# Two-layer decoder trunk: every fourth gate/up weight chunk gets its low part from ScalarE's negated high part and an accumulating transfer

## The chip, the core and the metric

One core of a Trainium2 chip runs the whole program: TensorE (PE in the profile) multiplies, VectorE (DVE), ScalarE (ACT) and GpSimd (POOL) work on tiles in SBUF and PSUM, SyncE (SP) issues most transfers, and 16 DMA engines carry them. The metric is the device time of one execution in microseconds (us); lower is better.

## The reference, cut to what matters

```python
def swiglu(h, w_gate, w_up, w_down):
    return (jax.nn.silu(h @ w_gate) * (h @ w_up)) @ w_down
...
for i in range(DEPTH):                  # DEPTH = 2
    h = rms_norm(x, norm_mix[i])
    x = x + mix                         # gla_mixer in layer 0, fox_mixer in layer 1
    h = rms_norm(x, norm_ffn[i])
    x = x + swiglu(h, ffn_w_gate[i], ffn_w_up[i], ffn_w_down[i])
```

`x` has 256 rows of 2048 float32 values. `w_gate` and `w_up` are 2048 x 5632, `w_down` is 5632 x 2048. All weights are float32 and each is read from HBM once.

## The kernel before

**A chunk.** Weights stream through four slots in SBUF. A chunk is 256 rows by 512 columns of a weight matrix (512 KB), laid out as 128 partitions x 1024 floats. Chunk c lives in slot c mod 4 of three buffers: `raw` (as loaded), `w_hi` (rounded to the reduced format `F32R` that TensorE reads in one pass) and `w_lo` (`raw - w_hi`, the remainder). The activations are split the same way (`xt_hi`, `xt_lo`), and each product is made of three matmuls, hi x hi, hi x lo and lo x hi, so a chunk costs TensorE 2 x 2 x 3 = 12 matmuls of 512 columns.

**The steps of a chunk, and what orders them.** Every engine's list is written out by hand and runs in order; semaphores connect them.

1. SP (`load`, L271) issues the load of a chunk into `raw[slot]` once `lo_done` says that the chunk four before it has had its low part made. That is the moment at which `raw[slot]` is free.
2. ACT (`hi`, L603) waits for the load to land and for `chunk_used` of the chunk four before (its `w_hi` and `w_lo` slot is then free), and writes `w_hi[slot]`.
3. DVE (`lo`, L1003) waits for `hi_done` and writes `w_lo[slot]` by a subtraction; `lo_done` rises by 1.
4. PE (`tile`, L358 to L360) waits for `lo_done`, does its 12 matmuls into `acc`, and raises `chunk_used`.

**The gate/up stage.** For layer 0 and layer 1 a SwiGLU has 11 column blocks (`FT`) of 512. A block is a gate tile of 8 chunks and then an up tile of 8 chunks. Around the chunks, ACT applies Silu to the gate sums (L705, after the third `hi` of the up tile), DVE multiplies by the up sums (L1126) and transposes the result in pieces (L1063), and ACT and DVE split it into `ht_hi` and `ht_lo` (L656, L1072). POOL has nothing to do in these blocks. After block 10 (blocks count from 0) comes the layer's down projection. Over both layers these are 352 gate/up chunks and 176 down chunks, the mixers have the other 288, and the program has 816.

Of the kernel before, what the change touches and what calls it, by code (L numbers as in the profile page):

```python
# [76 lines left out]
def build(nc, x, norm_mix, norm_ffn, gla_w_in, gla_w_g2, gla_b_g2, gla_o_gain, gla_w_o,  # L77
# [39 lines left out]
    with ctx:  # L117
# [137 lines left out]
        neg_made = sem("causal_mask_made")  # L255
        fv_done, og_done, pv_mm, rec_done = sem("fox_v_done"), sem("og_done"), sem("pv_product"), sem("rec_done")

        block = ctx.enter_context(nc.Block())

        GAIN_MIX0, GAIN_MIX1, GAIN_FFN0, GAIN_FFN1, GAIN_O, BIAS_G, GAIN_QK = 0, 16, 32, 48, 64, 68, 76  # L260
# [3 lines left out]
        @block.sync  # L264
        def _(sp):
            def load(src, row, col, c, j):

                slot = j % SLOTS

                wait(sp, lo_done, c + (j - SLOTS + 1))  # L270
                sp.dma_start(  # L271
                    raw[:, slot, :].rearrange("p (k n) -> p k n", n=N),
                    src[row:row + KC_CHUNK * P, bass.ds(col, N) if not isinstance(col, int) else slice(col, col + N)]
                    .rearrange("(k p) n -> p k n", p=P)).then_inc(landed[slot], 16)

            def project(src, col0, tiles, c0):

                with sp.Fori(0, tiles // 2) as i:
                    for j in range(2 * CH):
                        load(src, j % CH * KC_CHUNK * P, i * (2 * N) + (col0 + j // CH * N),  # L280
                             Lin(c0, 2 * CH, i), j)

            def swiglu(layer, c_up, c_down):
                with sp.Fori(0, FT) as i:
                    for j in range(2 * CH):
                        load((w_gate, w_up)[j // CH][layer], j % CH * KC_CHUNK * P, i * N,
                             Lin(c_up, 2 * CH, i), j)
                with sp.Fori(0, DT // 2) as i:
                    for j in range(2 * HCH):
                        load(w_down[layer], j % HCH * KC_CHUNK * P, i * (2 * N) + j // HCH * N,  # L290
                             Lin(c_down, 2 * HCH, i), j)

            def load_x(h):
                s = slice(h * KC_CHUNK * P, (h + 1) * KC_CHUNK * P)
                sp.dma_start(xres[:, :, s], x[0, :, s].rearrange("(b p) n -> p b n", p=P)) \
                    .then_inc(x_landed[h], 16)

            x_before = {0: (0,), 1: (1,), 2: (2,), 3: (3,), 4: (4, 5), 5: (6,), 6: (7,)}
            for j in range(2 * CH):
                for h in x_before.get(j, ()):  # L300
                    load_x(h)
                load(gla_w_in[0], j % CH * KC_CHUNK * P, j // CH * N, Lin(C["gla_in"]), j)
            project(gla_w_in[0], 2 * N, 2 * QT + 2 * DT - 2, C["gla_in"] + 2 * CH)
            project(gla_w_o[0], 0, DT, C["gla_o"])
            swiglu(0, C["ffn0"], C["down0"])
            project(fox_w_in[0], 0, 3 * DT, C["fox_in"])
            project(fox_w_in[0], 3 * D + FH, DT, C["fox_in"] + 3 * DT * CH)
            project(fox_w_o[0], 0, DT, C["fox_o"])
            swiglu(1, C["ffn1"], C["down1"])
            for b in range(TB):  # L310
                sp.wait_ge(staged, G["ffn1"] + FT + DT + b)
                sp.dma_start(out[0, b * P:(b + 1) * P, (DT - 1) * N:DT * N], stage[:, b, :]).then_inc(last_stored, 16)
            sp.wait_ge(last_stored, 16 * TB)
# [3 lines left out]
        def _(pe):  # L317
# [9 lines left out]
                last.then_inc(turned, 1)  # L327

            def tile(pair, c, off, hi, lo, chunks=CH, turn_n=None, mid=None, before=None, ready=None,
                     rows_first=False, second=ident):  # L330


                for j in range(chunks):
                    if before is not None:
                        before(j)
                    if ready is not None and j == chunks - 2:
                        pe.wait_ge(tp_hi, ready)
                        pe.wait_ge(tp_lo, ready)
                    if j == 4:
                        if turn_n is not None:  # L340
                            turn(turn_n, second)
                        if mid is not None:
                            mid()
                    if j == 6 and turn_n is not None:
                        wait(pe, tp_hi, turn_n + 1)
                        wait(pe, tp_lo, turn_n + 1)
                    slot = (c.base + off + j) % SLOTS
                    wait(pe, lo_done, c + (off + j + 1))
                    order = [(r, b) for r in range(KC_CHUNK) for b in range(TB)]
                    if rows_first and j == chunks - 1:  # L350
                        order = [(r, b) for b in range(TB) for r in range(KC_CHUNK)]
                    for r, b in order:
                        k = j * KC_CHUNK + r
                        wh = w_hi[:, slot, r * N:(r + 1) * N]
                        wl = w_lo[:, slot, r * N:(r + 1) * N]
                        o = acc[:, pair, b, :]
                        xh, xl = hi[:, k, b * P:(b + 1) * P], lo[:, k, b * P:(b + 1) * P]
                        pe.matmul(o, xh, wh, start=(k == 0), stop=False)  # L358
                        pe.matmul(o, xh, wl, start=False, stop=False)  # L359
                        last = pe.matmul(o, xl, wh, start=False, stop=(k == chunks * KC_CHUNK - 1))  # L360
                        if rows_first and j == chunks - 1 and (r, b) == (KC_CHUNK - 1, 0):
                            last.then_inc(rows_summed, 1)
                    last.then_inc(chunk_used, 1)
# [20 lines left out]
            def out_and_ffn(c_o, g_o, c_up, g_up, c_down, g_down, second):  # L384
# [6 lines left out]
                tile(1, Lin(c_up), CH, xt_hi, xt_lo)  # L391
                with pe.Fori(1, FT) as i:
                    cc = Lin(c_up, 2 * CH, i)
                    tile(0, cc, 0, xt_hi, xt_lo)
                    tile(1, cc, CH, xt_hi, xt_lo)

                pe.wait_ge(tp_hi, g_up + FT - 1)
                pe.wait_ge(tp_lo, g_up + FT - 1)
# [190 lines left out]
        def _(ac):  # L589
# [12 lines left out]
                wait(ac, chunk_used, cj + (1 - SLOTS))  # L602
                nc.scalar.activation(w_hi[:, slot, :], raw[:, slot, :], ACT.Copy).then_inc(hi_done, 1)  # L603

            def tile(c, off, empty, turned_tile=None, mid=None, chunks=CH, after_8=None, swapped_tile=None):

                for j in range(3):
                    hi(c, off + j)
# [1 line left out]
                    empty()  # L610
                for j in range(3, 7):
                    hi(c, off + j)
                if turned_tile is not None:
                    turned_tile()
                if mid is not None:
                    mid()
                hi(c, off + 7)
                if swapped_tile is not None:
                    swapped_tile()
                if chunks > CH:  # L620
# [68 lines left out]
            def out_and_ffn(c_o, g_o, c_up, g_up, c_down, g_down, norm, first, first_turn, after):  # L689
# [19 lines left out]
                tile(Lin(c_up), CH, lambda: silu(None))  # L709
                with ac.Fori(1, FT) as i:  # L710
                    cc = Lin(c_up, 2 * CH, i)
                    tile(cc, 0, None)
                    tile(cc, CH, lambda: silu(i), lambda: turn_h(Lin(g_up - 1, 1, i), Lin(-1, 1, i)))
                for t in range(DT):
                    if g_down is None and t:
                        tile(Lin(c_down), t * HCH, None, chunks=HCH)
# [274 lines left out]
        def _(ve):  # L991
# [5 lines left out]
                chain[0] += 1  # L997
                ve.wait_ge(dve_chain, chain[0])

            def lo(c, j):  # L1000
                slot = (c.base + j) % SLOTS
                wait(ve, hi_done, c + (j + 1))
                nc.vector.tensor_tensor(w_lo[:, slot, :], raw[:, slot, :], w_hi[:, slot, :].bitcast(F32),  # L1003
                                        ALU.subtract).then_inc(lo_done, 1)

            def tile(c, off, empty=None, turned_tile=None, mid=None, chunks=CH, late=None, swaps=None, after_8=None,
                     swapped_tile=None):
                for j in range(8):
                    lo(c, off + j)
                    if j == 2 and empty is not None:  # L1010
                        empty()
                    if j == 3 and late is not None:
# [89 lines left out]
            def out_and_ffn(c_o, g_o, c_up, g_up, c_down, g_down, m, norm, first, first_turn, saved):  # L1102
# [34 lines left out]
                def up_swaps(n):  # L1137
                    return lambda j: swap_h(n, 10 + 2 * j, 2) if j < 3 else None

                tile(Lin(c_up), 2 * CH, lambda: hidden(Lin(0)), swaps=gate_swaps(Lin(g_up)))  # L1140
                tile(Lin(c_up), 3 * CH, None, lambda: turn_h(Lin(g_up), Lin(0)), swaps=up_swaps(Lin(g_up)))
                with ve.Fori(2, FT) as i:
                    cc = Lin(c_up, 2 * CH, i)
                    n = Lin(g_up - 1, 1, i)
                    tile(cc, 0, lambda: hidden(Lin(-1, 1, i)), swaps=gate_swaps(n))
                    tile(cc, CH, None, lambda: turn_h(n, Lin(-1, 1, i)), swaps=up_swaps(n))
                for t in range(DT):
                    if t == 0:
                        n = Lin(g_up + FT - 1)
# [338 lines left out]
        def _(po):  # L1488
# [28 lines left out]
                nc.gpsimd.tensor_copy(xres[:, :, t * N:(t + 1) * N], stage[:, :, :]).then_inc(x_saved, 1)  # L1517


            link(nc.gpsimd.memset(ident[:, :], 0.0))  # L1520
            nc.gpsimd.affine_select(out=ident[:, :], in_=ident[:, :], compare_op=ALU.not_equal, fill=1.0, base=0,
                                    pattern=[[-1, P]], channel_multiplier=1).then_inc(ident_made, 1)
# [43 lines left out]
            for t in range(DT):  # L1566
                save(G["gla_o"] + t, t)
            x_rstd(1)
            for t in range(DT):
                save(G["down0"] + t, t)  # L1570
            po.wait_ge(chunk_used, C["fox_in"])
# [44 lines left out]
            for t in range(DT):  # L1616
                save(G["fox_o"] + t, t)
            x_rstd(3)
            for t in range(DT - 1):
                po.wait_ge(staged, G["ffn1"] + FT + t + 1)  # L1620
                po.dma_start(out[0, :, t * N:(t + 1) * N].rearrange("(b p) n -> p b n", p=P), stage[:, :, :]) \
# [24 lines left out]
```

## Time and profile before

| | |
|---|---|
| time of three runs | 2316.53, 2316.86, 2317.07 us; median 2316.86 |
| the profiled execution | span 2314.9 us from its first to its last instruction; no separate time is listed for it, so it stands 1.96 us below the median |
| PE busy | 2307.5 us (100%) |
| DVE / ACT / POOL busy | 1505.4 (65%) / 1099.5 (47%) / 167.9 (7%) us |
| transfers | 435.80 MB, mean 188 GB/s |

The profile is of one execution. Busy time counts compute instructions alone. "Idle before" is the time for which an engine stood still just before an instruction, and the name behind the arrow is the instruction whose semaphore ended that. Matmuls overlap in the pipeline, so the duration of one is longer than the distance between two starts.

### The profile page before, as it was taken

What the parts mean: (1) busy time and instruction counts of PE and PEld (TensorE: products, weight loads), DVE (VectorE), ACT (ScalarE), POOL (GpSimd) and SP (SyncE); (2) the same over time, 40 slices, a digit from 0 to 9 for tenths busy, and PEclk for the clock granted to TensorE, in tenths of its full rate; (3) what the DMA queues carried; (4) which work ended last, traced back from release to release, by engine and by line L of the source; (5) the groups of instructions that cost most, each with busy time, mean ns of one, the idle gap of its engine ahead of it and who ended that gap; (6) DMA issues with size and microseconds to landing.
All of it is one profiled execution on the core that took longest, in us unless ns stands there. A gap on an engine that the chain in (4) does not pass through costs nothing.

```text
span 2314.9 us, 29817 instructions
## 1 busy us (share of the span) xinstructions
PE 2307.5 (100%) x10416; PEld 1911.8 (83%) x10416; DVE 1505.4 (65%) x1883; ACT 1099.5 (47%) x1417; POOL 167.9 (7%) x206
## 2 busy tenths in 40 slices
PE   9999999999999999999999999999999999999999
PEld 7888788888888888888888888888888888888887
DVE  6988468566666666666578756577666666675443
ACT  6544554444444444444566656445444444444333
POOL 2036110000000000000223200001000000000000
PEclk9999999999999999999999999999999999999999
DMA  7655545666666665555656655455666666656654
GB/s 216 196 168 165 163 164 185 206 192 195 193 190 192 196 190 192 195 195 191 186 169 219 206 178 164 155 179 196 197 193 189 198 191 190 197 191 203 204 198 142
DMA packets 229932, 435.80 MB, mean 188 GB/s; under 512 B 17604, under 2 KB 19752, under 8 KB 229848
## 3 DMA queue, kind: packets, MB, share of 16 engines
q1 hardware_dynamic: 224416, 430.49, 58.6%
q0 software_dynamic: 1040, 3.69, 0.4%
q10 hardware_dynamic: 4392, 0.50, 0.2%
q8 instruction: 53, 0.87, 0.2%
q14 instruction: 31, 0.25, 0.0%
HBM read 432.52 MB, written 2.11 MB: 188 GB/s over the span
## 4 chain that ended last, share of the span: by engine, by line
PE 98%; DVE 1%; ACT 1%; issue 0%; ACTq 0%; POOL 0%; POOLq 0%; DVEq 0%
PE acc L358 32%; PE acc L360 31%; PE acc L359 31%; PE wk L483 1%; DVE w_lo L1003 0%; PE tp L325 0%; PE wk L540 0%; PE tp L550 0%; DVE fox_qkT L1369 0%; ACT w_hi L603 0%; PE wk L372 0%; PE wk L371 0%; PE wk L567 0%; PE wk L568 0%; PE wk L566 0%
## 5 line engine op out<-in xcount | busy, mean ns | idle before, releaser
L1003 DVE TENSOR_TENSOR w_lo<-raw,w_hi 128x1024 fp32r<-128x1024 f32 x816 | 1010.7, 1248 | 665.9 <-ACT w_hi L603 663.4
L603 ACT ACTIVATE w_hi<-raw 128x1024 fp32r<-128x1024 f32 x816 | 858.8, 1060 | 971.2 <-PE acc L360 935.5
L358 PE MATMUL acc<-w_hi,xt_hi 128*128 128x512 f32 x2304 | 902.8, 392 | 2.3 <-DVE w_lo L1003 2.2
L360 PE MATMUL acc<-w_hi,xt_lo 128*128 128x512 f32 x2304 | 896.8, 389 | 0.0
L359 PE MATMUL acc<-w_lo,xt_hi 128*128 128x512 f32 x2304 | 896.6, 389 | 0.0
L358 PEld LDWEIGHTS acc<-w_hi,xt_hi 128*128 128x128 f32 x2304 | 432.5, 188 | 95.6 <-DVE w_lo L1003 3.1
L360 PEld LDWEIGHTS acc<-w_hi,xt_lo 128*128 128x128 f32 x2304 | 432.4, 188 | 90.4
L359 PEld LDWEIGHTS acc<-w_lo,xt_hi 128*128 128x128 f32 x2304 | 432.6, 188 | 89.5 <-issue 1.0
L358 PE MATMUL acc<-w_hi,ht_hi 128*128 128x512 f32 x704 | 273.9, 389 | 0.0
L359 PE MATMUL acc<-w_lo,ht_hi 128*128 128x512 f32 x704 | 273.9, 389 | 0.0
L360 PE MATMUL acc<-w_hi,ht_lo 128*128 128x512 f32 x704 | 273.9, 389 | 0.0
L1063 DVE STREAM_TRANSPOSE ht_raw<-stage 32x256 f32<-32x256 f32 x496 | 216.2, 436 | 9.4
L360 PEld LDWEIGHTS acc<-w_hi,ht_lo 128*128 128x128 f32 x704 | 132.1, 188 | 27.5
L358 PEld LDWEIGHTS acc<-w_hi,ht_hi 128*128 128x128 f32 x704 | 132.1, 188 | 27.4
L359 PEld LDWEIGHTS acc<-w_lo,ht_hi 128*128 128x128 f32 x704 | 132.1, 188 | 27.4
L358 PE MATMUL acc<-w_hi,yt_hi 128*128 128x512 f32 x256 | 99.9, 390 | 0.0
L360 PE MATMUL acc<-w_hi,yt_lo 128*128 128x512 f32 x256 | 99.6, 389 | 0.0
L359 PE MATMUL acc<-w_lo,yt_hi 128*128 128x512 f32 x256 | 99.6, 389 | 0.0
L1517 POOL COPY xres<-stage 128x1024 f32<-128x1024 f32 x12 | 12.5, 1045 | 1076.1 <-DVE stage L1039 1076.1
L1369 DVE STREAM_TRANSPOSE fox_qkT<-stage 32x256 f32<-32x256 f32 x128 | 55.8, 436 | 8.3 <-ACT stage L908 6.3
L359 PEld LDWEIGHTS acc<-w_lo,yt_hi 128*128 128x128 f32 x256 | 48.1, 188 | 10.0
L360 PEld LDWEIGHTS acc<-w_hi,yt_lo 128*128 128x128 f32 x256 | 48.0, 188 | 10.0
(204 smaller groups left out, 935.6 us busy)
## 6 DMA issues: line engine op xcount, KB each, us to landing
raw<-in_ffn_w_gate_dram SPq DMA_DIRECT2D x176, 512.0 KB, 4.3
raw<-in_ffn_w_up_dram SPq DMA_DIRECT2D x176, 512.0 KB, 3.6
raw<-in_ffn_w_down_dram SPq DMA_DIRECT2D x176, 512.0 KB, 4.6
raw<-in_fox_w_in_dram SPq DMA_DIRECT2D x128, 512.0 KB, 4.9
raw<-in_gla_w_in_dram SPq DMA_DIRECT2D x96, 512.0 KB, 4.5
raw<-in_gla_w_o_dram SPq DMA_DIRECT2D x32, 512.0 KB, 4.2
raw<-in_fox_w_o_dram SPq DMA_DIRECT2D x32, 512.0 KB, 3.6
xres<-in_x_dram SPq DMA_DIRECT2D x8, 256.0 KB, 6.5
```

Of the source, the lines that this page charges most:

```text
L358: pe.matmul(o, xh, wh, start=(k == 0), stop=False)
L359: pe.matmul(o, xh, wl, start=False, stop=False)
L360: last = pe.matmul(o, xl, wh, start=False, stop=(k == chunks * KC_CHUNK - 1))
L483: last = pe.matmul(wk[:, b, h * P:(h + 1) * P], ks, qs, start=(kf == 0), stop=(kf == FPH - 1))
L603: nc.scalar.activation(w_hi[:, slot, :], raw[:, slot, :], ACT.Copy).then_inc(hi_done, 1)
L1003: nc.vector.tensor_tensor(w_lo[:, slot, :], raw[:, slot, :], w_hi[:, slot, :].bitcast(F32), ALU.subtract).then_inc(lo_done, 1)
L1063: last = nc.vector.transpose(dst[32 * j:32 * j + 32, :, :, 32 * i:32 * i + 32], src[32 * i:32 * i + 32, :, :, 32 * j:32 * j + 32])
L1369: last = nc.vector.transpose(dst[32 * j:32 * j + 32, :, :, 32 * i:32 * i + 32], src[32 * i:32 * i + 32, :, :, 32 * j:32 * j + 32])
L1517: nc.gpsimd.tensor_copy(xres[:, :, t * N:(t + 1) * N], stage[:, :, :]).then_inc(x_saved, 1)
```

## The change

In gate/up blocks 1 to 10 of both layers, the chunks in slot 3 (every fourth) get their low part in another way. ACT, right after `w_hi`, writes minus the high part of `raw` into `w_lo` (`minus`, the same Copy with scale -1). POOL waits for it and issues a transfer from `raw[3]` to `w_lo[3]` with accumulation, which adds `raw` to what stands there. DVE leaves these chunks out and raises `lo_done` by 2 at slot 2 to keep the count. PE waits for `lo_added` ahead of such a chunk, and SP waits for it before it loads over `raw[3]`, and once before the down projection. SP's loop over the blocks is written out, since its waits are on constants.

```diff
             def swiglu(layer, c_up, c_down):
-                with sp.Fori(0, FT) as i:
+                for i in range(FT):
                     for j in range(2 * CH):
+                        if j % SLOTS == LAST and (i, j) >= (1, 2 * SLOTS - 1):
+                            sp.wait_ge(lo_added, 16 * ((layer * (FT - 1) + i - 1) * ROUNDS + j // SLOTS))
                         load((w_gate, w_up)[j // CH][layer], j % CH * KC_CHUNK * P, i * N,
-                             Lin(c_up, 2 * CH, i), j)
+                             Lin(c_up + 2 * CH * i), j)
+                sp.wait_ge(lo_added, 16 * (layer + 1) * (FT - 1) * ROUNDS)
...
                 for j in range(chunks):
+                    if by_dma is not None and j % SLOTS == LAST:
+                        wait(pe, lo_added, by_dma(off + j))
...
+            def minus(c, j):
+
+                if j % SLOTS == LAST:
+                    nc.scalar.activation(w_lo[:, LAST, :], raw[:, LAST, :], ACT.Copy, scale=-1.0).then_inc(minus_hi, 1)
...
                 for j in range(3, 7):
                     hi(c, off + j)
+                    if by_dma:
+                        minus(c, j)
...
                 hi(c, off + 7)
+                if by_dma:
+                    minus(c, 7)
...
                 for j in range(8):
-                    lo(c, off + j)
+                    if not by_dma:
+                        lo(c, off + j)
+                    elif j % SLOTS != LAST:
+                        lo(c, off + j, 2 if j % SLOTS == LAST - 1 else 1)
...
+            def add_low(layer):
+
+                for k in range((FT - 1) * ROUNDS):
+                    po.wait_ge(minus_hi, layer * (FT - 1) * ROUNDS + k + 1)
+                    po.dma_start(w_lo[:, LAST, :].bitcast(F32), raw[:, LAST, :], accum_op=ALU.add).then_inc(lo_added, 16)
...
             x_rstd(1)
+            add_low(0)
...
             x_rstd(3)
+            add_low(1)
```

`LAST` is 3 and `ROUNDS` is 4, so each layer has 10 x 4 = 40 such chunks, 80 in all.

On ACT, in the loop over blocks 1 to 10, the rows of the first four chunks of a gate tile were these before; a row that holds `chunk_landed_3` is the wait for slot 3's load.

```order
L74 REGISTER_ALU [waits chunk_landed_2]
L603 ACTIVATE w_hi<-raw 128x1024 [waits chunk_used]
L74 REGISTER_ALU [waits chunk_landed_3]
L603 ACTIVATE w_hi<-raw 128x1024 [waits chunk_used]
L74 REGISTER_ALU
L74 REGISTER_ALU [waits chunk_landed_0]
L603 ACTIVATE w_hi<-raw 128x1024 [waits chunk_used]
```

In the changed kernel the same place reads:

```order
L74 REGISTER_ALU [waits chunk_landed_2]
L616 ACTIVATE w_hi<-raw 128x1024 [waits chunk_used]
L74 REGISTER_ALU [waits chunk_landed_3]
L616 ACTIVATE w_hi<-raw 128x1024 [waits chunk_used]
L621 ACTIVATE w_lo<-raw 128x1024
L74 REGISTER_ALU
L74 REGISTER_ALU [waits chunk_landed_0]
L616 ACTIVATE w_hi<-raw 128x1024 [waits chunk_used]
```

The one added row, L621, stands right behind slot 3's high part and waits for nothing of its own.

On SP, the end of a layer's gate/up loads and the first down load now read as follows; before, each of the slot-3 loads waited for `lo_done` alone, and the branch row waited for nothing.

```order
L278 DMA raw<-in_ffn_w_up_dram 128x2x512 [waits lo_done] x3
L278 DMA raw<-in_ffn_w_up_dram 128x2x512 [waits lo_done,low_added]
L298 UNCONDITIONAL_BRANCH [waits low_added]
L298 ISA
L278 ISA [waits lo_done]
L278 DMA raw<-in_ffn_w_down_dram 128x2x512
```

Every fourth load stands behind `low_added` (the name of `lo_added` in the program), with three more loads queued behind it, and the down loads stand behind the last of a layer.

On POOL, between the last step of the reciprocal root for the FFN's norm and the copies of the down projection, the changed kernel has one new group:

```order
L1529 TENSOR_SCALAR psc<-psc 128x2 [waits pool_chain]
L1530 TENSOR_TENSOR rstd<-psc 128x2 [waits pool_chain]
L1550 DMA w_lo<-raw 128x1024 [waits minus_high_made] x40
L1543 COPY xres<-stage 128x2x512 [waits staged] x4
L1605 MEMSET fox_wn 128x848 [waits chunk_used]
```

These 40 transfers are alone on POOL while they run; the copies behind them wait for the down projection, which comes later in any case.

## Rows read from the trace of the kernel before

**Rows 1.** The page: busy time, and the chain that ended last
```profile
PE 2307.5 (100%) x10416; PEld 1911.8 (83%) x10416; DVE 1505.4 (65%) x1883; ACT 1099.5 (47%) x1417; POOL 167.9 (7%) x206
...
PE 98%; DVE 1%; ACT 1%; issue 0%; ACTq 0%; POOL 0%; POOLq 0%; DVEq 0%
```

**Rows 2.** Stretches: busy time of each engine, granted clock, DMA share, GB/s
```profile
core 0: us, PE busy (x) PEld busy (x) DVE busy (x) ACT busy (x) POOL busy (x), PEclk, DMA share, GB/s
400.00:860.00 460.00, 460.00 (x2034) 380.69 (x2033) 304.39 (x366) 202.48 (x208) 5.20 (x9) 1.00 0.63 195
```

**Rows 3.** Timeline, ACT, inside a gate tile and into the up tile
```profile
500.41 1.06 ACT L603 ACTIVATE w_hi<-raw 128x1024 fp32r<-128x1024 f32 x1 [1.66 <-PE acc L360]
503.13 1.06 ACT L603 ACTIVATE w_hi<-raw 128x1024 fp32r<-128x1024 f32 x1 [1.66 <-PE acc L360]
505.85 1.06 ACT L603 ACTIVATE w_hi<-raw 128x1024 fp32r<-128x1024 f32 x1 [1.66 <-PE acc L360]
508.57 1.06 ACT L603 ACTIVATE w_hi<-raw 128x1024 fp32r<-128x1024 f32 x1 [1.66 <-PE acc L360]
511.37 1.27 ACT L705 ACTIVATE act<-acc,rstd 128x512 f32<-128x512 f32 x2 [1.74 <-PE acc L360]
512.53 1.06 ACT L603 ACTIVATE w_hi<-raw 128x1024 fp32r<-128x1024 f32 x1
```

**Rows 4.** Timeline, DVE, the same stretch
```profile
498.79 1.23 DVE L1003 TENSOR_TENSOR w_lo<-raw,w_hi 128x1024 fp32r<-128x1024 f32 x1 [0.58 <-ACT w_hi L603]
501.50 1.23 DVE L1003 TENSOR_TENSOR w_lo<-raw,w_hi 128x1024 fp32r<-128x1024 f32 x1 [0.57 <-ACT w_hi L603]
```

**Rows 5.** Timeline, SP's queue, the same stretch
```profile
500.04 0.37 SPq L271 DMA_DIRECT2D raw<-in_ffn_w_up_dram  x1
502.76 0.37 SPq L271 DMA_DIRECT2D raw<-in_ffn_w_up_dram  x1
```

**Rows 6.** The tile raw, 440 to 860 us: loads' time from issue to landing
```profile
DMA to landing us min/median/max: 3.3/4.3/4.8
```

**Rows 7.** The lines that store out_dram from POOL, and their landing
```profile
L1621 POOL DMA_DIRECT2D out_dram<-stage x3: 725/730/845, 2133.5 to 2253.1; - x3
...
DMA to landing us min/median/max: 4.3/4.4/4.5
```

**Rows 8.** The other POOL transfers and their landing, each by its line
```profile
L1605 POOL DMA_DIRECT2D minus_c<-fox_z x1: 759/759/759, 1226.4 to 1226.4; - x1
...
DMA to landing us min/median/max: 4.2/4.2/4.2
...
L1592 POOL DMA_DIRECT2D fox_bias<-minus_c x4: 612/627/633, 1243.8 to 1309.0; - x4
...
DMA to landing us min/median/max: 6.9/7.7/8.3
```

**Rows 9.** The page: DMA queues, packets, MB, share of 16 engines; then the stretch 10 to 15 us
```profile
q1 hardware_dynamic: 224416, 430.49, 58.6%
...
10.00:15.00 5.00, 5.00 (x25) 4.09 (x24) 2.35 (x4) 2.45 (x6) 0.00 (x0) 1.00 1.07 392
```

**Rows 10.** Stretches in which PE has gaps: PE busy, granted clock
```profile
0.00:5.00 5.00, 3.39 (x15) 3.00 (x16) 0.19 (x1) 1.49 (x2) 3.21 (x13) 1.00 0.54 153
2310.00:2315.00 5.00, 1.42 (x7) 0.84 (x5) 1.39 (x2) 0.00 (x0) 0.00 (x0) 0.92 0.27 105
```

**Rows 11.** Waits in all: engine and line, waited for, us, times, longest
```profile
ACT w_hi L603 <- PE acc L360: 935.5, 620, 4.1
DVE w_lo L1003 <- ACT w_hi L603: 663.4, 563, 6.1
...
PEld acc L358 <- DVE w_lo L1003: 3.1, 6, 1.4
...
PE acc L358 <- DVE w_lo L1003: 2.2, 4, 1.0
```

More of the change, by code:

```diff
@@ L256, in build, with added @@
         fv_done, og_done, pv_mm, rec_done = sem("fox_v_done"), sem("og_done"), sem("pv_product"), sem("rec_done")
+        minus_hi, lo_added = sem("minus_high_made"), sem("low_added")
+        LAST = SLOTS - 1
+        ROUNDS = 2 * CH // SLOTS
+        def added(layer, i, j):
+            return Lin((layer * (FT - 1) - 1) * ROUNDS + j // SLOTS + 1, ROUNDS, i) * 16
         block = ctx.enter_context(nc.Block())
@@ L329, in tile @@
             def tile(pair, c, off, hi, lo, chunks=CH, turn_n=None, mid=None, before=None, ready=None,
-                     rows_first=False, second=ident):
+                     rows_first=False, second=ident, by_dma=None):
                 for j in range(chunks):
+                    if by_dma is not None and j % SLOTS == LAST:
+                        wait(pe, lo_added, by_dma(off + j))
                     if before is not None:
@@ L393, in out_and_ffn @@
                     cc = Lin(c_up, 2 * CH, i)
-                    tile(0, cc, 0, xt_hi, xt_lo)
-                    tile(1, cc, CH, xt_hi, xt_lo)
+                    by_dma = lambda j: added(int(g_down is None), i, j)
+                    tile(0, cc, 0, xt_hi, xt_lo, by_dma=by_dma)
+                    tile(1, cc, CH, xt_hi, xt_lo, by_dma=by_dma)
                 pe.wait_ge(tp_hi, g_up + FT - 1)
@@ L603, in hi, with tile @@
                 nc.scalar.activation(w_hi[:, slot, :], raw[:, slot, :], ACT.Copy).then_inc(hi_done, 1)
-            def tile(c, off, empty, turned_tile=None, mid=None, chunks=CH, after_8=None, swapped_tile=None):
+            def minus(c, j):
+                if j % SLOTS == LAST:
+                    nc.scalar.activation(w_lo[:, LAST, :], raw[:, LAST, :], ACT.Copy, scale=-1.0).then_inc(minus_hi, 1)
+            def tile(c, off, empty, turned_tile=None, mid=None, chunks=CH, after_8=None, swapped_tile=None,
+                     by_dma=False):
                 for j in range(3):
@@ L711, in out_and_ffn @@
                     cc = Lin(c_up, 2 * CH, i)
-                    tile(cc, 0, None)
-                    tile(cc, CH, lambda: silu(i), lambda: turn_h(Lin(g_up - 1, 1, i), Lin(-1, 1, i)))
+                    tile(cc, 0, None, by_dma=True)
+                    tile(cc, CH, lambda: silu(i), lambda: turn_h(Lin(g_up - 1, 1, i), Lin(-1, 1, i)), by_dma=True)
                 for t in range(DT):
@@ L998, in link, with lo @@
                 ve.wait_ge(dve_chain, chain[0])
-            def lo(c, j):
+            def lo(c, j, chunks=1):
                 slot = (c.base + j) % SLOTS
@@ L1003, in lo @@
                 nc.vector.tensor_tensor(w_lo[:, slot, :], raw[:, slot, :], w_hi[:, slot, :].bitcast(F32),
-                                        ALU.subtract).then_inc(lo_done, 1)
+                                        ALU.subtract).then_inc(lo_done, chunks)
             def tile(c, off, empty=None, turned_tile=None, mid=None, chunks=CH, late=None, swaps=None, after_8=None,
-                     swapped_tile=None):
+                     swapped_tile=None, by_dma=False):
                 for j in range(8):
-                    lo(c, off + j)
+                    if not by_dma:
+                        lo(c, off + j)
+                    elif j % SLOTS != LAST:
+                        lo(c, off + j, 2 if j % SLOTS == LAST - 1 else 1)
                     if j == 2 and empty is not None:
@@ L1138, in up_swaps @@
                     return lambda j: swap_h(n, 10 + 2 * j, 2) if j < 3 else None
-                tile(Lin(c_up), 2 * CH, lambda: hidden(Lin(0)), swaps=gate_swaps(Lin(g_up)))
-                tile(Lin(c_up), 3 * CH, None, lambda: turn_h(Lin(g_up), Lin(0)), swaps=up_swaps(Lin(g_up)))
+                tile(Lin(c_up), 2 * CH, lambda: hidden(Lin(0)), swaps=gate_swaps(Lin(g_up)), by_dma=True)
+                tile(Lin(c_up), 3 * CH, None, lambda: turn_h(Lin(g_up), Lin(0)), swaps=up_swaps(Lin(g_up)), by_dma=True)
                 with ve.Fori(2, FT) as i:
@@ L1144, in out_and_ffn @@
                     n = Lin(g_up - 1, 1, i)
-                    tile(cc, 0, lambda: hidden(Lin(-1, 1, i)), swaps=gate_swaps(n))
-                    tile(cc, CH, None, lambda: turn_h(n, Lin(-1, 1, i)), swaps=up_swaps(n))
+                    tile(cc, 0, lambda: hidden(Lin(-1, 1, i)), swaps=gate_swaps(n), by_dma=True)
+                    tile(cc, CH, None, lambda: turn_h(n, Lin(-1, 1, i)), swaps=up_swaps(n), by_dma=True)
                 for t in range(DT):
```

## The prediction

> **What bounds the kernel now.** I read the page first. PE is busy 100% of the span and holds 98% of the chain that ended last [rows 1], so nothing is won unless PE's own work shrinks, and this change takes no matmul away. Then the stretch of the first gate/up stage, 400 to 860 us: PE busy 460.00 of 460.00 us, clock 1.00, DMA engines 63% busy, DVE 304 us and ACT 202 us [rows 2]. DVE has a third of its time free where it is to be relieved. Then the waits of the whole program: ACT's high part waits for PE (935.5 us in all) and DVE's low part for ACT (663.4 us), while PE waits for a low part for 3.1 and 2.2 us [rows 11]. The low parts are never late.
>
> Then the timeline, for the clockwork of a chunk. ACT's high parts start at 500.41, 503.13, 505.85, 508.57, each released by PE [rows 3]: 2.72 us a chunk, 10.88 us for a round of four slots. A high part takes 1.06 us. DVE starts 0.03 us after one ends (501.47 to 501.50) and takes 1.23 us [rows 3, 4]; SP issues the next load into that slot 0.02 us after the low part (500.02 to 500.04) [rows 4, 5]; it lands 4.3 us later by the median, 3.3 at least, 4.8 at most [rows 6]. So a raw slot's loop is now 1.06 + 0.03 + 1.23 + 0.02 + 4.3 = 6.64 us, in a period of 10.88: 4.2 us of slack. The other limit is PE's: w_lo of a slot is free when the high part starts and needed three chunks later, 8.16 us; it is ready after 2.32.
>
> **The change part by part.**
>
> *DVE* loses 80 subtractions of 1.23 us, 98 us. They lie under PE's work and nothing waited for them, so this is worth 0. The count raised by 2 at slot 2 even frees the waits on `lo_done` a little earlier, for a load that now waits for the transfer anyway.
>
> *ACT* gains 80 Copies of the shape of L603, 1.06 us each, 85 us. In the stage ACT has 258 of 460 us free [rows 2], and its next high part comes 1.66 us after the last ended [rows 3]; the added 1.06 fits in there. Worth 0. In the up tile Silu stands ahead of slot 3 and pushes its high part by 1.27 us [rows 3], of which more below.
>
> *SP* loses its loop registers and gains waits; an issue is 0.37 us [rows 5] in 2.72. Worth 0 by itself. What counts is what stands behind a wait: three more loads.
>
> *The transfer* is the unknown. Call D the time from the end of ACT's negated part to PE and SP seeing the data added. The two loops of slot 3 become:
>
> - PE's limit: 1.06 + 1.06 + 0.03 + D ≤ 8.16, so D up to 6.0 us is hidden.
> - The raw slot: high part 1.06, minus part 1.06, hop 0.03, D, hop 0.02, load 4.3, and about 0.03 for ACT to see it: 6.5 + D ≤ 10.88, so D up to 4.4 us is hidden (5.4 if a load takes the 3.3 of the minimum). This is the tighter one. Beyond it, every round of four chunks lasts 6.5 + D.
>
> Do the loads of slots 0 to 2 get late behind SP's wait? They are issued in a burst when the transfer lands, and the first is needed by ACT only 2 x 2.72 us later and by PE a whole round later, so slot 3 stays the narrow place. Silu's 1.27 us falls between PE's end of slot 3 (2.72 us after the transfer lands) and the landing of the next load (4.3 us after it): 2.72 + 1.27 = 3.99, covered.
>
> D is not in the trace: no transfer there accumulates or stays in SBUF. From below: POOL's store of 512 KB to HBM takes 4.3 to 4.5 us from issue to landing, 0.73 of them POOL's own instruction [rows 7]; its 16 KB store takes 4.2 [rows 8], so nearly all of that is a fixed cost. A load from SP shows that 3.3 is possible for 512 KB [rows 6]; I take 3.3 as the lower end. From above: POOL's transfers into `fox_bias`, 512 KB landing in SBUF, take up to 8.3 us [rows 8]; with a second stream to read, below, 11.6. For the likely value I start from the store, which is nearest (same queue, same bytes, the same load stream beside it), 4.3 us, and add the second operand. An addition in the transfer has to read `raw` and `w_lo`, 512 KB more. The engines spend 0.586 x 2314.9 us on 430.49 MB [rows 9], 1.65 us per 512 KB; at 392 GB/s, the fastest stretch, it would be 1.34 us [rows 9]. Sharing the engines with the loads can double it to 3.3. I take 2.0. D = 6.3 us.
>
> The Trainium skill (Collectives: The Full Stack, The bandwidth ceiling: the fold count and why AG ≠ RS ≠ AR) says that a transfer that adds is slower because it reads two sources through one ring, and halves the rate. No row here shows it. By it the second stream costs as much again as the first.
>
> The sum. The loop is 6.5 + 6.3 = 12.8 us in place of 10.88: 1.92 us per round. Each layer has 40 of them; the first of a layer starts with its raw slot already loaded and meets only PE's limit, 6.3 - 6.0 = 0.3 us. So 78 x 1.92 + 2 x 0.3 = 150 us.
>
> *The wait ahead of the down projection.* SP lets no down load go before the last transfer of the layer has landed. At that moment PE, held by the same transfer, starts its last up chunk, 2.72 us. The first down chunk is ready 0.02 + 4.3 + 0.03 + 1.06 + 0.03 + 1.23 = 6.7 us after it. PE stands for 4.0 us, twice: 8 us. Were D short enough to be hidden, this wait would stay: the transfer lands 2.15 + D after the last high part starts, the down chunk is ready 6.7 us on, and PE has work for 10.88, so PE stands for D - 2.0 us, or 2.3 us per layer at D = 4.3.
>
> Together 158 us. Against the profiled execution 2314.9 + 158 = 2473; 1.96 us more for the median of the runs: **2475 us**.
>
> **The rivals.**
>
> *1. The transfer is hidden.* D is 4.4 us or less, the load is back in time, and only the two waits ahead of the down projections are left: 2 x (D - 2.0), at D = 4.3 4.6 us, 2321 us; at D = 3.3 2.6 us, 2319. It decides at D = 4.4, a tenth of a us above the store's 4.3. For it: the store's time is mostly fixed [rows 7, 8], an SBUF target may answer sooner than HBM, and the fastest stretch moves twice the bytes of this stage [rows 2, 9]. Against: a second operand must be read, and the instruction that makes more descriptors may be longer than 0.73. The Trainium skill (DMA: Bandwidth & Descriptors, Anatomy of one DMA) puts a POOL-issued transfer at 2.0 us and its bytes at 436 GB/s, 3.2 us for this size. The store's 4.3 stands above that. Chance 0.20, of which 0.13 are within 0.2% of before (4.6 us, about what a measurement of this kernel can tell from no change).
>
> *2. The adding path is much slower than copying, or PE's gaps cost clock too.* At D = 11.6 a round is 18.1 us, + 7.2 x 80 + 2 x 4 = 585 us, 2900. With a longer stand than the 1.9 us of the forecast, PE may also restart at the lower of its clocks: the last stretch, with 1.42 us of 5 busy, has 0.92; the first, with 3.39 of 5, still 1.00 [rows 10]. A chunk at 1.2 GHz costs 2.72 us more, and it stands partly in slot 3's loop (PE must free `w_hi` before the next high part, 5.44 us after the transfer lands in place of 2.72, where the load lands at 4.3): 1.1 us more per round, 90 us in all, 2565 at D = 6.3. Chance of ending above 2700, that is D over 9.1 or both together: 0.12.
>
> *3. The relief of DVE pays.* It would, if some low part were late now; PE's waits for low parts are 5.3 us in the whole program [rows 11], and not one of them can be more than that. Chance 0.02 of faster.
>
> The forecast's own case, D between 4.4 and 9.1, has 0.66.
>
> **How the numbers follow.** The predicted time is that of D = 6.3. Its own range is 2330 (D near 4.5) to 2700 (D = 9.1: 4.7 x 80 + 8). For 8 in 10 I reach down to no change, 2316, which takes in rival 1, and leave out what lies above 2700. Faster 0.02, within 0.2% 0.13, slower 0.85.
>
> **What would show it.** Landing of the 80 transfers on POOL (6.3 us from the end of L621; under 4.4 is rival 1, over 9 rival 2). PE's idle time ahead of L370 put down to the transfer or to POOL, near 1.9 us 78 times; starts of slot 3's chunk 12.8 us apart. SP's waits for the same transfers, and ACT's slot-3 high part released by a load's landing, no longer by PE. Two gaps of 4 us at the starts of the down projections. DVE's busy time down by 98 us, ACT's up by 85. The granted clock 1.00 in the gate/up stages. The mixers' and the down stages' lengths unchanged. The prediction is wrong if the second operand costs nothing, or if a load that comes in the burst behind the transfer lands later than 4.3 us, which would lengthen the round by as much.

## The result, and the profile after

| | before | changed |
|---|---|---|
| median of the runs | 2316.97 us | 2334.68 us (2334.09 to 2335.03) |
| span of the profiled execution | 2314.9 us | 2332.8 us |

The ratio is 1.0076, 95% interval 1.0062 to 1.0090. The change costs 17.7 us. It was forecast to cost 158. The direction was in the forecast, and so was the loss at the starts of the down projections (8 of the 158 us). The 150 us that it put into the gate/up rounds did not come.

From the page of the changed kernel, busy time first, then the chain that ended last [rows 1], then the transfer queues (packets, MB, share of 16 engines' span) [rows 9], then the issues of the new transfer with its median time to landing:

```profile
PE 2317.2 (99%) x10416; PEld 1912.8 (82%) x10416; DVE 1410.6 (60%) x1803; ACT 1171.8 (50%) x1497; POOL 236.6 (10%) x286
...
q1 hardware_dynamic: 224416, 430.49, 56.4%
q0 software_dynamic: 12560, 45.64, 9.5%
...
PE 95%; DMA 2%; ACT 1%; DVE 1%; issue 1%; ACTq 0%; POOL 0%; SPq 0%; POOLq 0%
...
w_lo<-raw POOLq DMA_DIRECT2D x80, 512.0 KB, 4.4
```

DVE lost 95 us of work and nothing came of it. The adding transfer lands 4.4 us after its issue, as fast as the plain store of the same size did [rows 7]. Through the gate/up stage PE is still busy 420.00 of 420.00 us, with the engines of the transfers at 0.78 in place of 0.63 [rows 2]. Busy time does not show a stand of 0.1 us there, since the row of a matmul (0.39 us) is longer than the distance between two starts; such stands are read from the starts. Just behind the stage there is a hole, and the granted clock is 0.83. Stretches of the changed kernel:

```profile
core 0: us, PE busy (x) PEld busy (x) DVE busy (x) ACT busy (x) POOL busy (x), PEclk, DMA share, GB/s
440.00:860.00 420.00, 420.00 (x1846) 345.45 (x1845) 234.62 (x303) 217.09 (x219) 32.91 (x38) 1.00 0.78 237
880.00:900.00 20.00, 16.60 (x62) 13.12 (x61) 13.57 (x20) 7.41 (x7) 0.00 (x0) 0.83 0.71 240
```

**Where the time went: two places.** The first is the start of the down projection. ACT's timeline there, POOL's transfer with SP's first down load, and PE's timeline, changed kernel:

```profile
869.84 1.06 ACT L616 ACTIVATE w_hi<-raw 128x1024 fp32r<-128x1024 f32 x1 [1.66 <-PE acc L372]
...
873.51 1.06 ACT L616 ACTIVATE w_hi<-raw 128x1024 fp32r<-128x1024 f32 x1 [1.66 <-DMA raw<-in_ffn_w_up_dram]
874.48 1.04 ACT L621 ACTIVATE w_lo<-raw 128x1024 fp32r<-128x1024 f32 x1
884.58 1.06 ACT L616 ACTIVATE w_hi<-raw 128x1024 fp32r<-128x1024 f32 x1 [9.05 <-DMA raw<-in_ffn_w_down_dram]
```

```profile
875.81 0.86 POOL L1550 DMA_DIRECT2D w_lo<-raw  x1 [9.74 <-ACT w_lo L621]
...
880.50 0.38 SPq L278 DMA_DIRECT2D raw<-in_ffn_w_down_dram  x1
```

```profile
883.24 0.39 PE L372 MATMUL acc<-w_hi,xt_lo 128*128 128x512 f32 x1
887.03 0.77 PE L370 MATMUL acc<-w_hi,ht_hi 128*128 128x512 f32 x1 [3.40 <-DVE w_lo L1026]
887.60 0.63 PE L371 MATMUL acc<-w_lo,ht_hi 128*128 128x512 f32 x1
888.03 0.63 PE L372 MATMUL acc<-w_hi,ht_lo 128*128 128x512 f32 x1
...
892.72 0.59 PE L371 MATMUL acc<-w_lo,ht_hi 128*128 128x512 f32 x1
893.14 0.40 PE L372 MATMUL acc<-w_hi,ht_lo 128*128 128x512 f32 x1
893.38 0.39 PE L370 MATMUL acc<-w_hi,ht_hi 128*128 128x512 f32 x1
```

The last adding transfer is issued at 875.81 and lands 4.4 us later; only then does SP issue the first down load (880.50), ACT waits 9.05 us for it, and PE starts its first down chunk 3.79 us after its last up matmul where 0.227 us is the pace. Then 13 matmuls start 0.43 us apart in place of 0.227, at 1.2 GHz in place of 2.4. That is 3.6 + 2.8 us for layer 0. In layer 1 the same hole is 3.7 us and the slow stretch shorter, 1.5 us: five starts 0.43 us apart, though PE's idle time before it is as long. Together 11.6 us.

```profile
2088.25 0.77 PE L370 MATMUL acc<-w_hi,ht_hi 128*128 128x512 f32 x1 [3.50 <-DVE w_lo L1026]
```

The second is small and comes once per block. ACT in an up tile of the changed kernel, and PE at the slot-3 chunk behind it:

```profile
511.82 1.27 ACT L728 ACTIVATE act<-acc,rstd 128x512 f32<-128x512 f32 x2 [1.74 <-PE acc L372]
512.98 1.06 ACT L616 ACTIVATE w_hi<-raw 128x1024 fp32r<-128x1024 f32 x1
513.93 1.06 ACT L621 ACTIVATE w_lo<-raw 128x1024 fp32r<-128x1024 f32 x1
```

```profile
519.48 0.39 PE L372 MATMUL acc<-w_hi,xt_lo 128*128 128x512 f32 x1
519.79 0.49 PE L370 MATMUL acc<-w_hi,xt_hi 128*128 128x512 f32 x1
520.12 0.40 PE L371 MATMUL acc<-w_lo,xt_hi 128*128 128x512 f32 x1
520.35 0.39 PE L372 MATMUL acc<-w_hi,xt_lo 128*128 128x512 f32 x1
```

Silu stands ahead of the high part. The negated part ends at 514.99, POOL issues at 515.28, the data land 4.4 us later at 519.7, and PE wanted them at 519.71 (519.48 + 0.227). Starts are 0.31 and 0.33 us apart there: about 0.2 us lost, in each of 20 blocks. With one larger stand of 0.9 us in layer 1 these make some 5 us.

### The profile page after: what moved, and what is told of

Read it like the earlier page. It is cut to its first block, busy times and chain, and to the rows that moved or that the text cites. A ratio compares the mean times of both kernels' runs of the same rounds, so it can differ in the third digit from the quotient of the medians.

```text
span 2332.8 us, 29127 instructions
## 1 busy us (share of the span) xinstructions
PE 2317.2 (99%) x10416; PEld 1912.8 (82%) x10416; DVE 1410.6 (60%) x1803; ACT 1171.8 (50%) x1497; POOL 236.6 (10%) x286
## 4 chain that ended last, share of the span: by engine, by line
PE 95%; DMA 2%; ACT 1%; DVE 1%; issue 1%; ACTq 0%; POOL 0%; SPq 0%; POOLq 0%
PE acc L370 31%; PE acc L371 30%; PE acc L372 30%; DMA w_lo<-raw 1%; PE wk L496 1%; DVE w_lo L1026 1%; DMA raw<-in_ffn_w_up_dram 1%; ACT w_hi L616 0%; PE tp L335 0%; DMA raw<-in_ffn_w_down_dram 0%; PE wk L553 0%; ACT w_lo L621 0%; PE tp L563 0%; DVE fox_qkT L1395 0%; PE wk L384 0%
## 5 line engine op out<-in xcount | busy, mean ns | idle before, releaser
L1026 DVE TENSOR_TENSOR w_lo<-raw,w_hi 128x1024 fp32r<-128x1024 f32 x736 | 913.2, 1251 | 779.1 <-ACT w_hi L616 776.4
L1550 POOL DMA_DIRECT2D w_lo<-raw x80 | 69.6, 869 | 863.2 <-ACT w_lo L621 863.2
L621 ACT ACTIVATE w_lo<-raw 128x1024 fp32r<-128x1024 f32 x80 | 83.7, 1047 | 0.0
```

Of the source, the lines that this page charges most:

```text
L621: nc.scalar.activation(w_lo[:, LAST, :], raw[:, LAST, :], ACT.Copy, scale=-1.0).then_inc(minus_hi, 1)
L1550: po.dma_start(w_lo[:, LAST, :].bitcast(F32), raw[:, LAST, :], accum_op=ALU.add).then_inc(lo_added, 16)
```

## The experiments

In each of them the kernel before ran on the same chip: 2316.92 us in the first four, 2317.17 us in the last three.

**The wait ahead of the down projection (e1_down_wait).**

```diff
-                sp.wait_ge(lo_added, 16 * (layer + 1) * (FT - 1) * ROUNDS)
                 with sp.Fori(0, DT // 2) as i:
                     for j in range(2 * HCH):
+                        if j == LAST:
+                            sp.wait_ge(lo_added, 16 * (layer + 1) * (FT - 1) * ROUNDS)
                         load(w_down[layer], j % HCH * KC_CHUNK * P, i * (2 * N) + j // HCH * N,
                              Lin(c_down, 2 * HCH, i), j)
```

> The changed kernel, except that SP's wait for the last added low part of a layer stands ahead of the fourth down load (the first that writes raw[3]) and no longer ahead of the first. Theory A (most of the loss is at the two starts of the down projection: PE stands 3.5 us and then runs 14 matmuls at half clock, 3 us more): 13 us come back, 2321.5 us, no gap ahead of the first down chunk, clock 1.00 there. Theory B (the loss is spread over the gate/up rounds, since the raw slot's round of 6.5 us + D is longer than 10.88): at most 3 us come back, 2331 us or more, and the gap moves to another chunk.

Measured: 2323.41 us, ratio to before 1.0028 (1.0017 to 1.0040). 11.3 us came back, against 13 expected and 11.6 read from the trace. From 860 to 900 us PE is busy 39.97 of 40.00 us at clock 1.00, in this kernel's stretch:

```profile
860.00:900.00 40.00, 39.97 (x175) 32.50 (x174) 24.65 (x34) 18.96 (x20) 1.72 (x2) 1.00 0.73 229
```

Theory A holds. The 6.5 us by which it is still slower than before are the stands of the second place, among them layer 1's larger one of 0.9 us and one more of 0.8 us at the end of its gate/up stage. The loads of slots 0 to 2 never touch what the last transfer reads, so the wait belongs to the fourth.

**Silu behind slot 3 (e2_silu_later).**

```diff
-                for j in range(3):
+                for j in range(4 if by_dma else 3):
                     hi(c, off + j)
+                    if by_dma:
+                        minus(c, j)
                 if empty is not None:
                     empty()
-                for j in range(3, 7):
+                for j in range(4 if by_dma else 3, 7):
                     hi(c, off + j)
-                    if by_dma:
-                        minus(c, j)
```

> The changed kernel, except that in blocks 1 to 10 ACT makes slot 3's high and negated part ahead of Silu, not behind it. Theory A (in each of the 20 blocks Silu's 1.27 us push the transfer just over the 8.16 us that PE's limit allows, and PE stands 0.22 us): 4.4 us come back, 2330.3 us, and the small stand ahead of the fourth up chunk is gone. Theory B (the stand comes from the load of raw[3] being late, not from Silu): no change, 2334.7 us, and the stand stays.

Measured: 2327.09 us, ratio to before 1.0042 (1.0029 to 1.0056). 7.6 us came back where 4.4 were expected. PE of this kernel goes through the same place at its pace:

```profile
519.39 0.39 PE L372 MATMUL acc<-w_hi,xt_lo 128*128 128x512 f32 x1
519.61 0.39 PE L370 MATMUL acc<-w_hi,xt_hi 128*128 128x512 f32 x1
519.84 0.39 PE L371 MATMUL acc<-w_lo,xt_hi 128*128 128x512 f32 x1
```

The stand was Silu's doing (theory A). The other 3 us stand elsewhere in the trace. The larger stand in layer 1 is 0.3 us in place of 0.9. The hole ahead of layer 0's down projection is 2.67 us in place of 3.40, as PE's idle time shows, and behind it 8 matmuls run at half clock in place of 13, 1.2 us less:

```profile
884.20 0.47 PE L370 MATMUL acc<-w_hi,ht_hi 128*128 128x512 f32 x1 [2.67 <-DVE w_lo L1026]
```

The hole is shorter because the last high part is on time. In the changed kernel it started 3.67 us after the one before it (869.84 to 873.51), released by a load that had waited for the transfer behind Silu. Here it starts at the pace of 2.72 us, released by PE:

```profile
867.97 1.06 ACT L616 ACTIVATE w_hi<-raw 128x1024 fp32r<-128x1024 f32 x1 [1.66 <-PE acc L372]
...
870.69 1.06 ACT L616 ACTIVATE w_hi<-raw 128x1024 fp32r<-128x1024 f32 x1 [0.71 <-PE acc L372]
```

In layer 1 the high part is on time too, but its hole is still 3.6 us, since the first down load is used 5.1 us after the last transfer lands there (2073.2 to 2078.3), and 4.4 us in layer 0 of the changed kernel.

**Both (e3_both).** The two edits above together.

> Both edits in one: the wait ahead of the fourth down load and Silu behind slot 3's two parts. Theory A (these two places hold the whole loss, the transfer itself is hidden at 4.7 us): 2317.3 us, as before the change, with PE busy without a stand from 440 to 1060 us. Theory B (the round of slot 3 is too long in itself, or the added traffic slows loads elsewhere): 2325 us or more.

Measured: 2317.34 us, ratio to before 1.0002 (0.9993 to 1.0011). Nothing of the loss is left beyond what the measurement can tell, about 2 us, so the two places hold all of it. The page of this kernel shows that 80 transfers still add up low parts and DVE still does 95 us less:

```profile
PE 2308.0 (100%) x10416; PEld 1911.6 (83%) x10416; DVE 1410.6 (61%) x1803; ACT 1172.3 (51%) x1497; POOL 238.5 (10%) x286
```

It is no faster than before either, as PE is what bounds both.

**A plain copy (e4_plain_copy).**

```diff
-                    po.dma_start(w_lo[:, LAST, :].bitcast(F32), raw[:, LAST, :], accum_op=ALU.add).then_inc(lo_added, 16)
+                    po.dma_start(w_lo[:, LAST, :].bitcast(F32), raw[:, LAST, :]).then_inc(lo_added, 16)
```

> The changed kernel with a plain transfer in place of the adding one: raw[3] is copied over w_lo[3], so 80 low parts are the whole weights and the output is another. It asks why the adding transfer lands after 4.4 us where 6.3 were forecast. Theory S (a second operand costs nothing, the fixed part is all): the copy lands after 4.4 us too, engines busy 2.65 us a transfer as now, time 2334.7 us. Theory T (the second operand costs 1.0 to 1.3 us, and a target in SBUF answers that much sooner than HBM): the copy lands after 3.1 to 3.4 us, engine time of a transfer 1.3 us in place of 2.65; the stands in the 20 blocks are gone and those at the down projections are 1.1 us shorter, 2322 to 2328 us.

Measured: 2320.82 us, ratio to before 1.0016 (1.0007 to 1.0025). POOL's line and its landing, first of the changed kernel:

```profile
L1550 POOL DMA_DIRECT2D w_lo<-raw x80: 852/863/1084, 448.6 to 2076.8; - x80
...
DMA to landing us min/median/max: 4.4/4.4/4.8
```

and then of the plain copy:

```profile
L1550 POOL DMA_DIRECT2D w_lo<-raw x80: 537/538/797, 448.4 to 2065.4; - x80
...
DMA to landing us min/median/max: 2.8/2.8/3.5
```

and the software queue on its page, 4.8% where the adding one has 9.5%:

```profile
q0 software_dynamic: 12560, 45.64, 4.8%
```

Theory T holds, and by more than its number: the copy lands after 2.8 us, where 3.1 to 3.4 were expected. So the addition costs 1.6 us of landing, 0.33 of them in POOL's own instruction (0.86 against 0.54). Its engine time: 0.095 x 2332.8 less the 9 us that the queue had before (0.4% of 2314.9) is 212 us, 2.65 per transfer; the copy has 0.048 x 2320.6 - 9 = 102 us, 1.28. An adding transfer works the engines twice as long as a copy of as many bytes. The time, 2320.8, lies just under the range expected, with holes of 1.7 and 2.0 us at the down projections and no stands in the blocks. In the profiled execution, which took 2322.3 us, eight matmuls at half clock stand behind the hole in layer 1, and none behind the one in layer 0:

```profile
2075.70 0.47 PE L370 MATMUL acc<-w_hi,ht_hi 128*128 128x512 f32 x1 [1.81 <-DVE w_lo L1026]
...
2070.00:2085.00 15.00, 13.19 (x52) 10.39 (x51) 10.03 (x14) 6.36 (x6) 0.00 (x0) 0.89 0.82 278
```


**A longer D (e5_delay_1, e6_delay_2).** On top of e3_both, one or two fills on POOL ahead of each transfer:

```diff
                     po.wait_ge(minus_hi, layer * (FT - 1) * ROUNDS + k + 1)
+                    for _ in range(1):      # 2 in e6_delay_2
+                        link(nc.gpsimd.memset(masks[:, :, :], 0.0))
                     po.dma_start(w_lo[:, LAST, :].bitcast(F32), raw[:, LAST, :], accum_op=ALU.add).then_inc(lo_added, 16)
```

> The kernel of e3_both (2317.3 us, nothing lost) with one fill of 128 x 1024 floats on POOL ahead of each of the 80 adding transfers; such a fill took 0.96 us before, with its semaphore about 1.05, so D goes from 4.7 to 5.75 us. Theory L (the round of the raw slot is the narrow limit, as the prediction had it; measured by the parts of the changed kernel it is 1.06 + 0.96 + D + 0.03 + 3.8 + 0.1 = 5.95 + D): a round of 11.7 us in place of 10.88, + 0.8 x 78, 2381 us. Theory P (only PE's limit matters, 1.06 + 0.96 + D up to 8.16): hidden, 2317 to 2319 us.

Measured: 2378.16 us, ratio to before 1.0262 (1.0247 to 1.0278).

> The same with two fills, D = 6.8 us, 0.5 us over the 6.3 of the prediction. Theory L: a round of 12.75 us, + 1.87 x 78 = 146, 2463 us, and an idle PE of 1.9 us ahead of each slot-3 chunk. Theory P: PE's own loop is 1.06 + 0.96 + 6.8 + 2.72 = 11.54 us, + 0.66 x 78 = 51, 2369 us. If PE's clock falls with the stands, up to 90 us more than either.

Measured: 2459.11 us, ratio to before 1.0615 (1.0599 to 1.0631). Theory L gave 2381 and 2463, theory P 2317 to 2319 and 2369. The second fill costs 81 us more, 1.01 us a round, which is what it adds to D. ACT's timeline in e6_delay_2, with slot 3's high parts released by the load that came after the transfer:

```profile
599.48 1.06 ACT L617 ACTIVATE w_hi<-raw 128x1024 fp32r<-128x1024 f32 x1 [4.32 <-DMA raw<-in_ffn_w_gate_dram]
600.45 1.04 ACT L622 ACTIVATE w_lo<-raw 128x1024 fp32r<-128x1024 f32 x1
...
612.04 1.06 ACT L617 ACTIVATE w_hi<-raw 128x1024 fp32r<-128x1024 f32 x1 [4.25 <-DMA raw<-in_ffn_w_gate_dram]
...
624.83 1.06 ACT L617 ACTIVATE w_hi<-raw 128x1024 fp32r<-128x1024 f32 x1 [4.26 <-DMA raw<-in_ffn_w_up_dram]
```

and POOL's beside it:

```profile
601.55 1.97 POOL L1552 MEMSET masks<- 128x1024 f32 x2 [9.68 <-ACT w_lo L622]
603.81 0.86 POOL L1553 DMA_DIRECT2D w_lo<-raw  x1 [0.30 <-POOL masks L1552]
```

D is 603.81 + 4.4 - 601.49 = 6.7 us, the rounds are 12.56 and 12.79 us, and (2459.1 - 2317.3) / 80 gives 1.77 us over 10.88, 12.65. So the loop of the raw slot is real, and its constant is 12.65 - 6.7 = 5.9 us. PE stands about 1.6 us in each round and keeps its clock through layer 0's stage:

```profile
440.00:860.00 420.00, 371.75 (x1599) 297.14 (x1597) 202.83 (x261) 188.24 (x191) 91.56 (x99) 1.00 0.68 206
```

It does not keep it everywhere. At 1932 us, behind one of layer 1's stands, two matmuls run at full pace and then eight at half clock, while a longer stand in layer 0 (at 506.73) has no such stretch behind it:

```profile
506.73 0.49 PE L371 MATMUL acc<-w_hi,xt_hi 128*128 128x512 f32 x1 [2.59 <-DMA w_lo<-raw]
...
1931.98 0.49 PE L371 MATMUL acc<-w_hi,xt_hi 128*128 128x512 f32 x1 [1.87 <-DMA w_lo<-raw]
...
1930.00:1940.00 10.00, 8.13 (x29) 6.50 (x29) 2.76 (x5) 4.45 (x6) 1.27 (x2) 0.83 0.74 236
```

**PE kept busy in the hole (e7_warm_gap).** On the changed kernel:

```diff
                 pe.wait_ge(tp_hi, g_up + FT - 1)
                 pe.wait_ge(tp_lo, g_up + FT - 1)
+                warm_up(28)
                 for t in range(DT):
```

> The changed kernel with 28 small matmuls of no use (128 columns, into a PSUM bank that is free there) on PE between the last up chunk and the first down chunk of each layer, 3.0 us at full clock, so they fit into the 3.5 us of the stand. Theory C (the stand is paid twice, once itself and once by 14 matmuls at half clock behind it): the stand for the first down chunk stays at its time, the half clock is gone, 6 us come back, 2328.7 us. Theory N (the clock falls for another reason or the extra matmuls only add): 2334.7 us or more.

Measured: 2329.47 us, ratio to before 1.0054 (1.0040 to 1.0068). PE's timeline:

```profile
883.74 3.22 PE L436 MATMUL wk<-ident 128*128 128x128 f32 x28
886.96 0.50 PE L370 MATMUL acc<-w_hi,ht_hi 128*128 128x512 f32 x1
887.30 0.40 PE L371 MATMUL acc<-w_lo,ht_hi 128*128 128x512 f32 x1
887.54 0.40 PE L372 MATMUL acc<-w_hi,ht_lo 128*128 128x512 f32 x1
```

The first down matmul starts when it did (886.96 against 887.03) and the ones behind it keep the full pace. Layer 1 has no slow stretch either. 5.2 us came back, near the 2.8 + 1.5 read as half clock in the changed kernel; layer 1's larger stand, 0.9 us there and 0.2 us here, is most of the difference. So theory C holds: that hole is paid twice, and the second part is the clock's.

## Why the prediction was wrong in size

- *PE bounds, and DVE's and ACT's part are worth nothing.* Right. DVE fell by 95 us (98 worked out), ACT rose by 72 (85), and e3_both stands at the time of before.
- *The loop of the raw slot is the narrow one, and beyond it each round is a constant plus D.* Right in kind, shown by e5_delay_1 and e6_delay_2. The constant was 6.5 and measured 5.9: the negated part runs straight behind the high part and adds 0.96, not 1.06, and a load issued when the transfer has just landed is used by ACT 3.9 us later (869.64 to 873.51), where the sum had the stage's median of 4.3 and two hops.
- *D = 6.3 us.* This term failed. Measured: 0.29 us from ACT to POOL's issue and 4.4 to landing, 4.7. It was made of 4.3 for the store [rows 7] and 2.0 for the second operand. The 2.0 was fair: the addition costs 1.6. The 4.3 was not. It was read from a store into HBM, and the same queue moves the same bytes inside SBUF in 2.8 us. The store differs from the copy in its target, and also in its place in the program; no run changes the target alone, so that the 1.5 us are the target's is argued and not shown, and a target in SBUF alone does not make a transfer quick, as the ones into `fox_bias` with 6.9 to 8.3 us show [rows 8]. I called the target's share a thing that speaks for rival 1 and gave it no number. And 5.9 + 4.7 = 10.6 is less than 10.88, so of the 150 us for the rounds none came. D was the larger of the two errors: with D = 6.3 and the right constant it would have been (12.2 - 10.88) x 78 = 103, with D = 4.7 and the constant of 6.5 still (11.2 - 10.88) x 78 = 25.
- *Silu is covered.* Wrong, though small. I checked its 1.27 us against the raw slot's loop alone, and not against PE's limit, where they come off the 6.0 us allowed to D: 4.7 us remain, and D is 4.7. Some 5 us in the changed kernel, shown by e2_silu_later.
- *The wait ahead of the down projection.* Right in place, near in size by luck. 8 us were forecast for both layers, and the holes are 7.2 us. But the 8 took PE as held by the transfer up to that point, which it was not; by the formula for a hidden transfer, 2 x (D - 2.0), they would be 5.4. The rest comes mostly from the last high part of a layer, which starts 0.9 us late in layer 0 and 0.8 us in layer 1 because it waited for its load. Not priced at all was the clock behind them, 4.3 us by the trace; e7_warm_gap brings back 5.2, some 0.7 of it from layer 1's larger stand. Only rival 2 had the clock fall, and in the gate/up rounds, where the changed kernel's stands are shorter and it did not fall.
- *Rival 1, the transfer hidden.* This is the case that came, and in part by luck: its own condition, D of 4.4 or less, was not met at D = 4.7, and the transfer is hidden only because the loop's constant was also 0.6 us too large. It expected 2321 us and missed the clock and Silu. The rule of the Trainium skill that stood beside it (DMA: Bandwidth & Descriptors, Anatomy of one DMA; 3.2 us for this size) lies between the copy's 2.8 and the adding transfer's 4.4. The other rule (Collectives: The Full Stack, The bandwidth ceiling: the fold count and why AG ≠ RS ≠ AR) is stated for ReduceScatter, a step that adds between several cores; the queue's engine time here, 2.65 against 1.28 us, agrees with it.
- *What was to be seen.* Foretold and seen: the holes at the down projections, DVE's fall, ACT's rise, the clock of 1.00 in the gate/up stages. Foretold and not seen: rounds of 12.8 us and PE idle in 78 of them.

e1_down_wait and e2_silu_later bring back 1.6 us more together than e3_both does (11.3 + 7.6 against 17.3). The traces show an overlap of about that size: the hole of layer 0 and the slow stretch behind it are 0.7 + 1.2 us shorter in e2_silu_later, and e1_down_wait brings back the same 1.9 us. What stays open is why layer 1's larger stand is 0.9 us in one kernel and 0.2 in another that does not touch it (e7_warm_gap).

## What to carry to other kernels

The price of a transfer to one memory need not hold for another: here it was 1.5 us too high. Take the nearest row of the same kind of source and target, and give "it may answer sooner" a number before leaning on the sum. A guard on a reused buffer belongs ahead of the first access to that buffer, not ahead of the whole next stage; one wait placed three loads too early held two thirds of this loss, and more than a third of that was clock. When a step gets longer, hold each instruction that stands ahead of it on its engine against every limit it feeds, in the worst round and not in the usual one.

## What the runs showed of the hardware

- A transfer within SBUF that adds, 512 KB from POOL: 4.4 us from issue to landing, 2.65 us of 16 engines' time, 0.86 us of POOL. The copy: 2.8, 1.28 and 0.54. The store to HBM: 4.3 to 4.5 [rows 7].
- TensorE's clock behind a single stand, by PE's idle time before it. Starts were 0.43 us apart (1.2 GHz) where 0.227 us is the full pace (2.4 GHz). Idle 3.40 us (changed kernel, layer 0): 13 such starts at once. Idle 3.50 us (changed kernel, layer 1) and 3.39 us (e2_silu_later, layer 1): 5 at once. Idle 2.67 us (e2_silu_later, layer 0): 5 matmuls at full pace and then 8 at 1.2 GHz, granted clock 0.83 over those ten us. Idle 1.81 us (e4_plain_copy, layer 1): 5 and then 8. Idle 1.57 us (e4_plain_copy, layer 0): none. Idle 1.87 us (e6_delay_2, at 1932 us): 2 and then 8, while idle 2.59 us in the same run had none, nor had the other stands of some 1.6 us in every 12.65 us. So the length of a stand alone does not tell whether the clock falls behind it.
